# A state update in a decoder-layer kernel: the old state is added by VectorE instead of multiplied by a unit matrix

## What is computed

```
def _wkv_step(S, inp):
    r, w, k, v, kk, b = inp
    sa = jnp.einsum('bhvk,bhk->bhv', S, -kk)
    S = S * w[:, :, None, :] + sa[..., :, None] * b[:, :, None, :] + v[..., :, None] * k[:, :, None, :]
    y = jnp.einsum('bhvk,bhk->bhv', S, r)
    return S, y
...
    S_T, y = lax.scan(_wkv_step, S0.astype(f32), (tm(r), tm(w), tm(k), tm(v), tm(kk), tm(kk * a)))
```

## Time and profile before

| what | value |
| --- | --- |
| median of 3 runs | 2074.05 us |
| lowest and highest | 2072.22 and 2077.15 us |
| the profiled execution | 2077.03 us |
| its span, first to last instruction | 2075.2 us |
| TensorE, VectorE, ScalarE busy | 83%, 29%, 13% of the span |
| one pair's period | 110.7 us |

### The profile page before, as it was taken

How to read it: one execution, slowest core, us unless ns; L and a number is a source line. 1 busy time by engine, 2 the same in 40 slices (tenths; PEclk the granted TensorE clock), 3 DMA queues, 4 the chain that set the end, 5 groups by cost and what they waited for, 6 DMA issues and landing times.

```text
span 2075.2 us, 26200 instructions
## 1 busy us (share of the span) xinstructions
PE 1721.0 (83%) x9068; PEld 1020.0 (49%) x9068; DVE 601.3 (29%) x1081; ACT 280.0 (13%) x539; POOL 124.1 (6%) x101
## 2 busy tenths in 40 slices
PE   7998989999999999899989677686867768676563
PEld 4776767677777677676764222231322323232111
DVE  6536363545454444530020111011111101011012
ACT  2221212222121212121140000000000000000001
POOL 0202011110102020200000000000000000000000
PEclk9999999999999999999988889797888889798886
DMA  7223222222131222237138999999999999999992
GB/s 275 97 75 110 75 93 74 105 75 96 65 109 66 84 96 85 76 122 259 61 142 335 421 421 421 422 422 422 422 422 422 422 422 422 422 422 422 422 421 92
DMA packets 91151, 510.36 MB, mean 246 GB/s; under 512 B 23424, under 2 KB 26624, under 8 KB 31776
## 3 DMA queue, kind: packets, MB, share of 16 engines
q1 hardware_dynamic: 91056, 509.61, 61.4%
q0 software_dynamic: 48, 0.12, 0.0%
HBM read 499.87 MB, written 9.82 MB: 246 GB/s over the span
## 4 chain that ended last, share of the span: by engine, by line
PE 56%; DMA 26%; DVE 11%; issue 3%; SPq 1%; ACT 1%; DVEq 1%; ACTq 0%
PE ps_PJ L587 16%; DMA arena<-w_up 15%; DVE arena L1209 11%; PE ps_C L895 8%; DMA arena<-w_gate 8%; PE ps_PJ L785 6%; PE ps_PJ L866 4%; DMA arena<-w_down 3%; PE ps_PJ L873 2%; PE ps_C L645 2%; PE ps_C L668 1%; ACT arena L963 1%; SPq L500 1%; PE ps_C L927 1%; PE ps_SB L927 1%
## 5 line engine op out<-in xcount | busy, mean ns | idle before, releaser
L587 PE MATMUL ps_PJ<-arena 128*128 128x320 f32 x1792 | 542.2, 434 | 4.0 <-ACTq L365 4.0
L895 PE MATMUL ps_C<-arena 128*32 128x512 f32 x2048 | 306.8, 754 | 148.6 <-DMA arena<-w_up 113.6
L587 PEld LDWEIGHTS ps_PJ<-arena 128*128 128x128 f32 x1792 | 319.8, 190 | 111.5 <-issue 11.6
L895 PEld LDWEIGHTS ps_C<-arena 128*32 128x32 f32 x2048 | 81.3, 134 | 368.5 <-issue 363.9
L1209 DVE TENSOR_TENSOR arena<-ps_PJ,arena 128x512 f32<-128x512 f32 x32 | 22.1, 692 | 655.1 <-PE ps_PJ L866 655.1
L963 ACT ACTIVATE arena<-ps_C 128x512 f32<-128x512 f32 (+1 forms) x68 | 46.2, 679 | 1119.5 <-PE ps_C L895 599.8
L1209 DVE TENSOR_TENSOR arena<-arena 128x320 f32<-128x320 f32 (+12 forms) x227 | 153.8, 677 | 45.3 <-ACTq L365 25.3
L1671 POOL TENSOR_TENSOR arena<-arena 128x640 f32<-128x640 f32 (+2 forms) x80 | 118.3, 1478 | 780.3 <-DVEq L365 422.9
L1209 DVE TENSOR_TENSOR arena<-arena,ps_PJ 128x512 f32<-128x512 f32 (+2 forms) x112 | 73.5, 657 | 292.5 <-PE ps_PJ L873 167.0
L785 PE MATMUL ps_PJ<-arena 128*128 128x320 f32 x512 | 146.4, 439 | 2.1 <-DVEq L365 2.1
L866 PE MATMUL ps_PJ<-arena 128*128 128x128 f32 (+1 forms) x768 | 140.6, 313 | 0.3 <-DVEq L365 0.3
(11 more groups left out here) (173 smaller groups left out, 1347.6 us busy)
## 6 DMA issues: line engine op xcount, KB each, us to landing
arena<-w_gate SPq DMA_DIRECT2D x128, 1024.0 KB, 19.0
arena<-w_up SPq DMA_DIRECT2D x128, 1024.0 KB, 18.6
arena<-w_down SPq DMA_DIRECT2D x128, 1024.0 KB, 18.8
arena<-win SPq DMA_DIRECT2D x59, 1024.0 KB, 4.8
arena<-w_out SPq DMA_DIRECT2D x16, 1024.0 KB, 8.4
arena<-xT SPq DMA_DIRECT2D x8, 640.0 KB, 6.9
arena<-s_ret SPq DMA_DIRECT2D x8, 512.0 KB, 3.9
o_sret<-arena SPq DMA_DIRECT2D x8, 512.0 KB, 3.9
```

The costliest lines, as they stand in the source:

```text
L587: last = mm(pj(j)[:, 0:T], wt[j % NSLOT][:, kt, :], hT[:, kt, :], start=kt == 0, stop=kt == KT - 1)
L895: last = mm((GB, UB)[u][h * CAP:(h + 1) * CAP, :], xg[:, kt, h * CAP:(h + 1) * CAP], w[h][:, k, :], start=kt == 0, stop=kt == KT - 1)
```

## The change

The unit matrix's product goes (24 of them: three chunks, eight pairs). For c = 1, 2, 3 VectorE adds bank C2 to S in place when TensorE has filled it, and signals with a new semaphore, `state_sum`. ScalarE waits for it, scales S in place, from SBUF to SBUF, and releases the bank as before. For c = 0 nothing changes. VectorE's addition stands where s{c} stands in the table, and the count of its late operations rises from 22 to 25.

```
-VCHAIN = [72, 22]
+VCHAIN = [72, 25]
...
-                    if c > 0:
-                        mm(b[:, 0:P], ident, S, start=True, stop=False)
-                    mm(b[:, 0:P], tok[:, 1, c, :], SA, start=c == 0, stop=False)
+                    mm(b[:, 0:P], tok[:, 1, c, :], SA, start=True, stop=False)
                     mm(b[:, 0:P], tok[:, 2, c, :], tok[:, 0, c, :], start=False, stop=True).then_inc(full(s), 1)
...
-                    A(S, bank(s)[:, 0:P], ACT.Copy, scale=wc(c)).then_inc(free(s), 1)
+                    if c > 0:
+                        act.wait_ge(done("state_sum"), 3 * p + c)
+                    A(S, S if c > 0 else bank(s)[:, 0:P], ACT.Copy, scale=wc(c)).then_inc(free(s), 1)
...
+                elif s in ("s1", "s2", "s3"):
+                    wait_filled(dve, s, p)
+                    TT(S, S, bank(s)[:, 0:P], ALU.add).then_inc(done("state_sum"), 1)
```

## The result

| | before | after |
| --- | --- | --- |
| median of 5 runs | 2072.78 us | 2104.53 us |
| lowest and highest | 2072.22 and 2077.15 us | 2100.90 and 2107.32 us |
| profiled execution, its span | 2077.03, 2075.2 us | 2104.53, 2102.7 us |
| a pair's distance, clock at 1.00 | 110.68 us | 113.62 us |
| a pair's distance, clock fallen | none fell | 115.30 us |

The changed kernel takes 1.0144 times as long (95% interval 1.0133 to 1.0156); the two medians are 31.8 us apart, which by themselves would be 1.0153. The forecast was 2103.3 us. The two profiled executions differ less, by 27.5 us, because that of the kernel before lay 4.3 us above its median and that of the changed kernel at it.

The account below looks back on a forecast made before the run. TensorE's order, ScalarE's square and VectorE's stretch bound the pairs, DMA the expert stage. Pairs and tail 20.8 us plus clock 8.4 gave 29.2: 2106.2 profiled, less 3.0 to the median, about 2103.3 us; range 2091 to 2113.

Parts of the forecast that it names:

- the one-for-one passage: Stage of pairs into expert stage: a later end starts the weights' stream, and moves the kernel's end, by as much.
- s1: First addition in a pair: hidden behind nearly 5 us of TensorE work; the dropped product gains 0.22 us a pair.
- s2: Second addition, behind VectorE's normalisation: delays ScalarE's scaling and square, so ss starts 2.70 us later a pair.
- s3: Third addition, inside VectorE's critical stretch between the shift of r and copy of y: 0.44 us a pair.
- The pair: One pair's sum over the three steps: 2.70 + 0.44 - 0.22 = 2.92 us longer.
- The tail: Eighth set's late steps, among output projection products: r3 waits for the scaling and u2 starts later, about +0.4 us.
- The clock: TensorE's longer gap before ss halves its granted clock in six of eight cases: 7 x 0.75 x 1.6 = 8.4 us.
- (a): Rival on TensorE's clock: it stays full despite the 3.30 us gap before ss; 2094.9 us, chance 0.23.
- (b): Rival on TensorE's clock: every stall before ss costs the dearer 2.48 us; 2112.3 us, chance 0.08.
- (c): Rival on the three steps: additions hide and the dropped products save 5.3 us; 2068.8 us, chance 0.03.
- (d): Rival on order at ss: square runs ahead of scaling, or ss is late anyway; 2075.6 us, chance 0.04.

Follow-up runs that it names:

- e9: Kernel before with VectorE's addition at s1 alone and ScalarE's square for ss ahead of the scaling of s2: 2066.83 us, 0.9971.
- e2: Kernel before with only the addition of s2 made by VectorE, s1 and s3 keeping the unit matrix's product: 2111.43 us, 1.0182.
- e1: Kernel before with only the addition of s1 made by VectorE, s2 and s3 keeping the unit matrix's product: 2071.25 us, 0.9982.
- e10: Changed kernel with s2's addition right behind the reciprocal of ms, ahead of its three other operations: 2083.11 us, 1.0046.
- e5: Changed kernel with ScalarE's square for ss moved ahead of the scaling of S at s2: 2077.34 us, 1.0014.
- e3: Kernel before with only the addition of s3 made by VectorE, s1 and s2 keeping the unit matrix's product: 2076.69 us, 1.0010.
- e8: Changed kernel with the unit matrix's product kept in the eighth pair's late steps alone: 2103.50 us, 1.0137.
- e4: Changed kernel with four unread products on TensorE ahead of its wait at ss: 2096.45 us, 1.0105.
- e11: e2 with four unread products on TensorE ahead of its wait at ss: 2094.76 us, 1.0100.
- e6: Kernel before, no additions, with ScalarE's square for ss moved ahead of the scaling of s2: 2071.44 us, 0.9986.

## Why the prediction was right, and where a term was off

**What bounds the stage, and the one-for-one passage.** Right. The last wait of the stage of pairs ends 30.24 us later (963.04 for 932.80), the long wait ahead of the experts' stage at 1109.72 for 1079.30, 30.42 later. The last products start 28.9 us later (2065.89 for 2036.96), and the end comes 27.5 later. That is not the stream taking up part of the delay. From the end of that long wait to the end of the span the thirteen traces have one of two lengths, 992.4 to 993.1 us (seven, the changed kernel and e9, the earliest of all, among them) or 995.3 to 996.1 (six, the kernel before and e2, the latest of all, among them), and the second goes with a lower granted clock. The stretches of the two kernels, columns as in the earlier trace rows:

```profile
1079.30:2075.18 995.88, 715.83 (x4106) 267.72 (x4106) 130.76 (x207) 51.47 (x69) 0.00 (x0) 0.83 0.95 396
1109.72:2102.75 993.03, 700.56 (x4106) 263.81 (x4106) 130.78 (x207) 51.46 (x69) 0.00 (x0) 0.85 0.96 397
```

What decides between the two lengths no run tells.

**s1: a gain of 0.22 a pair, the addition hidden.** Right (e1), and 0.10 more that was not foreseen.

**s2: 2.70.** Right: the wait is 3.31 where 3.30 stood in the prediction, thus 3.31 - 0.38 - 0.22 = 2.71, and every link is in its row, the scaling at 0.40 between its two bounds. e10 and e5 show the cause by moving one operation each: the addition's place on VectorE, and the square's place on ScalarE.

**s3: 0.44.** In e3 as forecast. In the changed kernel the addition's hand-over is 0.25 and not 0.15, so 0.54; the following idle time is 0.51 and not 0.61, which makes it 0.44 after all. A right sum, with two terms of 0.10 that cancel:

```profile
626.32 0.29 DVE L1209 TENSOR_TENSOR arena<-arena,ps_C 128x128 f32<-128x128 f32 x1
626.86 0.42 DVE L1209 COPY arena<-ps_YB 128x256 f32<-128x256 f32 x1 [0.24 <-DVE arena L1209]
...
629.67 0.45 DVE L1209 TENSOR_SCALAR arena<-arena 128x320 f32<-128x320 f32 x1 [0.51 <-DVEq L365]
```

**The pair: 2.92.** 113.61 to 113.63 where the clock stayed at 1.00, thus 2.93 to 2.95.

**The tail: 0.4. Wrong, mis-sized.** From the root of ms to the end of the stage the eighth set takes 2.8 us more. The prediction counted r3 by its own 0.44 us and put u2 right behind it. The rows of TensorE show what it left out:

```profile
947.11 0.46 PE L676 MATMUL ps_C<-arena 128*128 128x128 f32 x2 [1.98 <-ACTq L365]
947.40 0.39 PE L677 MATMUL ps_C<-arena 128*128 128x128 f32 x2
947.63 0.70 PE L783 MATMUL ps_PJ<-arena 128*128 128x320 f32 x2
948.17 1.57 PE L758 MATMUL ps_RT<-arena 128*128 128x512 f32 x2
```

Between r3 and u2 stands a product of the output projection (L783), 0.54 us, r3 starts 0.19 behind the scaling, and its two products take 0.52 us, so that u2 starts 6.59 us behind the root of ms (941.58) where it was 5.36 (919.48 and 914.12): 1.23 in place of 0.4. And behind the wait of 1.98 us for the scaling the clock fell:

```profile
949.00:950.00 1.00, 1.00 (x2) 0.36 (x2) 0.22 (x1) 0.00 (x0) 0.00 (x0) 0.50 0.00 0
```

It lacks 0.25, 0.50, 0.50 and 0.46 in the four stretches from 948 us on, 1.7 us together. 1.2 and 1.7 are 2.9, near the 2.8. e8, with neither the wait nor the fall, gives 2.55 of it back. The same wait of 1.98 us stands there in e2, e4, e5 and e11 too; a fall comes within 1.4 us behind it in the changed kernel and in e5 and not in the other three, so this fall does not follow every such wait. The prediction looked for gaps that lower the clock before ss alone.

**The clock: 8.4.** A fall was put at 1.6 and costs 1.68. Seven times 0.75 would be 5.25 falls; the profiled execution had four in the pairs, thus 6.7 us, and the one in the tail. So the sum by the trace is 7 x 2.93 + 4 x 1.68 + 2.8 = 30.0 us, for 30.24 measured at the end of the stage. By e4 the clock's part is 8.1 us in the medians, which would be four falls in the pairs and most of one in the tail. The number of falls is not fixed (four here, five in e8); how many the other executions had no trace tells.

**The number as a whole: near, and in part by luck.** At the end of the stage the sum of 29.2 was only 1.0 too small, because two errors worked against each other: the tail took 2.4 us more than its 0.4, the clock 1.7 less than its 8.4. And the step from the profiled executions to the medians was not what it was taken for. The forecast was 2106.2 us for the profiled execution, less 3.0 because that of the kernel before lay so far above its median. The changed kernel's took 2104.53, 1.7 less than the 2106.2, and lay at its median and not 3.0 above it; these two, 3.0 and 1.7, nearly cancel and leave the 1.2 us between 2103.3 and 2104.53.

**The rivals.** (a), the clock stays full, 2094.9: not so in the changed kernel, and e4, which makes it so, comes to 2096.45, 1.5 above it, of which 0.8 is the tail's later u2. (b), the dearer price: no pair of the changed kernel paid 2.48, but e2's paid 2.77 in every one, so what I gave 0.08 was not far. (c), the additions hide: at s1 alone. At s2 e10 shows that an addition 1.83 us earlier still comes too late. (d), the order doesn't bind: e5 shows that it does; with another order the time is 2077.34, near the 2075.6 named for it.

## What to carry to other kernels

Work moved to an idle engine stands behind all that this engine was told before it; find the operation it will stand behind, and then what stands behind it on the engine that waits. One short instruction that feeds the bottleneck, put ahead of the one that now waits, can return nearly all of the loss (27 of 32 us here), and of three equal replacements only the one that had slack on both sides was worth making. When TensorE gets a new wait of some 2 to 3 us, look at the granted clock behind it too, in the tail as well as in the loop.

## What was not expected of the hardware

**A fall of the clock has no single price.** Behind waits of 3.31 us before ss it came in four of seven pairs and cost 1.68 us; behind waits of 3.37 us before the same step it came in seven of seven and cost 2.77. In the changed kernel it begins 0.5 to 1.2 us behind the restart and lasts 3.4 us; in e2 it begins 1.3 us ahead of it and lasts 6.8. One addition was thereby slower than three (2111.43 and 2104.53 us). In e2 the seven falls begin within some 0.15 us of each other, counted from ss; what keeps them there, and what decides whether an equal wait is followed by a fall, was not tested.

**A hand-over on VectorE.** The idle time ahead of VectorE's first operation of pa, behind mu, is 0.61 us in the kernel before and in e6, which have no addition and 22 late operations on VectorE, and 0.51 in the changed kernel and in the ten other runs, with 23, 24 or 25; in e1 and e9 no addition is near it. In the pairs it is on the path, 0.10 us each. No run tells why.

**A read from SBUF is little dearer than one from PSUM on ScalarE.** The scaling of 128 columns takes 0.40 us for 0.37.
